# A decoder step on one core: decode states kept outside the weight ring and stored from GpSimd's queue, the last expert pair peeled, the final norm done tile by tile

## What is computed

```python
h = rms_norm(x, norm_mix); proj = h @ w_in
# 8 heads of gated DeltaNet: S_t = exp(g_t)(I - beta_t k_t k_t^T) S_{t-1} + beta_t k_t v_t^T, o_t = S_t^T q_t
# 8 heads of stick-breaking attention over the paged cache
x = x + concat(o_gdn, o_sb) @ w_out
logits = rms_norm(x, norm_ffn) @ router_w + router_b          # 32 experts, top 4, softmax gates
hu   = t[tok] @ w_up[e] + b_up[e]                             # 1024 -> 2048, gate and up interleaved
act  = (clip(up, -7, 7) + 1) * min(gate, 7) * sigmoid(1.702 * gate)
x = x + sum over experts of gate_e * (act @ w_down[e] + b_down[e])
y = x * rsqrt(mean(x * x) + eps) * norm_final                 # 256 prompt rows and 32 decode rows
```

## Time and profile before

| | us |
|---|---|
| median of 3 runs | 1422.4 |
| lowest, highest | 1418.89, 1425.12 |
| the profiled execution, its own time | 1421.34 |
| its span, first to last instruction | 1419.6 |
| PE busy in it | 1274.5 (90%) |
| DVE, ACT, POOL busy | 409.4, 257.7, 71.4 |
| HBM read, written | 459.67 MB, 3.70 MB |

### The profile page before, as it was taken

The page is one execution under the profiler, slowest core; times in us unless marked ns, Lnnn a source line. Parts: engine busy times, 40 slices in busy tenths (PEclk is TensorE's granted clock), DMA queues, the critical chain, the costliest instruction groups (busy, mean ns, idle before and its releaser), DMA issues. The chain is left out here.

```text
span 1419.6 us, 19928 instructions
## 1 busy us (share of the span) xinstructions
PE 1274.5 (90%) x7806; PEld 578.5 (41%) x7806; DVE 409.4 (29%) x930; ACT 257.7 (18%) x417; POOL 71.4 (5%) x124
## 2 busy tenths in 40 slices
PE   3999667697996899999999999999999999999995
PEld 3777454466944233333333333333333333333332
DVE  1740222245354223221322213222131221312223
ACT  2211291132222111010110201101011110111102
POOL 1400020003220000000000000000000000000000
PEclk8999897887997899999999999999999999999998
DMA  9444366861007799999999999999999999999993
GB/s 329 158 135 137 105 177 200 243 184 32 4 5 266 288 403 429 428 428 429 428 428 428 428 429 428 428 429 428 428 428 428 428 428 428 428 429 428 428 429 125
DMA packets 68787, 464.04 MB, mean 327 GB/s; under 512 B 16653, under 2 KB 16781, under 8 KB 44164
## 3 DMA queue, kind: packets, MB, share of 16 engines
q1 hardware_dynamic: 68740, 463.40, 80.8%
HBM read 459.67 MB, written 3.70 MB: 326 GB/s over the span
## 5 line engine op out<-in xcount | busy, mean ns | idle before, releaser
L1860 PE MATMUL bank<-ring,work 128*64 128x512 f32 x2048 | 451.0, 595 | 23.2 <-DMA ring<-in_w_up 23.2
L1860 PEld LDWEIGHTS bank<-ring,work 128*64 128x64 f32 x2048 | 149.1, 137 | 323.1 <-issue 323.1
L1877 PE MATMUL bank<-ring,work 128*64 128x512 f32 x1024 | 229.9, 597 | 10.8 <-DMA ring<-in_w_down 6.7
L1877 PEld LDWEIGHTS bank<-ring,work 128*64 128x64 f32 x1024 | 69.4, 137 | 149.5 <-issue 122.6
L404 PE MATMUL bank<-hT,ring 128*128 128x288 f32 x448 | 115.4, 415 | 11.2 <-PEq L263 10.6
L404 PEld LDWEIGHTS bank<-hT,ring 128*128 128x128 f32 x448 | 85.4, 194 | 34.7 <-issue 12.2
L2020 DVE TENSOR_SCALAR work<-bank 128x512 f32<-128x512 f32 x32 | 21.9, 685 | 257.8 <-PE bank L1860 257.8
L1935 ACT ACTIVATE work<-bank 128x1024 f32<-128x1024 f32 x16 | 16.4, 1024 | 392.1 <-PE bank L1814 392.1
L1992 DVE TENSOR_TENSOR X<-X,bank 128x512 f32<-128x512 f32 x68 | 46.8, 689 | 126.3 <-PE bank L1831 126.3
L2032 DVE COPY work<-bank 128x512 f32<-128x512 f32 x16 | 11.1, 692 | 215.3 <-PE bank L1877 215.3
L1831 PE MATMUL bank<-work 128*128 128x512 f32 x136 | 62.9, 605 | 0.9 <-ACT work L1961 0.9
(11 more groups left out here) (372 smaller groups left out, 1132.1 us busy)
## 6 DMA issues: line engine op xcount, KB each, us to landing
ring<-in_w_up SPq DMA_DIRECT2D x128, 2048.0 KB, 17.2
ring<-in_w_down SPq DMA_DIRECT2D x64, 2048.0 KB, 15.3
ring<-in_cache_k SPq DMA_DIRECT2D x64, 256.0 KB, 2.9
ring<-in_cache_v SPq DMA_DIRECT2D x64, 256.0 KB, 2.9
ring<-in_w_in SPq DMA_DIRECT2D x7, 2048.0 KB, 14.4
ring<-in_w_out SPq DMA_DIRECT2D x2, 2048.0 KB, 12.8
out<-work SPq DMA_DIRECT2D x4, 512.0 KB, 2.8
X<-in_x_prompt SPq DMA_DIRECT2D x1, 1024.0 KB, 5.1
```

The lines of the kernel that those rows point to most:

```text
L1860: ins = pe.matmul(bank[CAP * e:CAP * e + CAP, g, :], xT[:, k, CAP * e:CAP * e + CAP], weight(ch + e, k % 2 * RSLOT + 512 * g), start=False ...
L1877: ins = pe.matmul(bank[CAP * e:CAP * e + CAP, 4 + m, :], aT[:, k, CAP * e:CAP * e + CAP], weight(ch + e, k % 4 * D + 512 * m), start=False ...
```

## The change

In the mixer section `vm` moves out of the ring to a place in `work`, over constants that are not needed any more (`blk64`, which is, changes places with them), and the new decode states are written there too (`S1`), over the `vm` of the heads already used; the old states stay in the ring and are only read. SyncE's list loses the wait for `d_up`, the sixteen stores and the wait for them.

```diff
@@ -1030,15 +1030,16 @@
         assert f_ <= CONST_END, (f_, CONST_END)
         QK, wT, vn = (work[:, W * i:W * (i + 1)] for i in range(3))
         osq, ors, otm = Lb, Y, kbg
-        vm = ring[:, W:W + 2048].rearrange("p (h s d) -> p h s d", h=HP, s=NSEQ)
-        s_ssm = sem("ssm_stored")
+        vm = work[:, CONST_END:CONST_END + 2048].rearrange("p (h s d) -> p h s d", h=HP, s=NSEQ)
+        S1 = vm
+        s_ssm, s_sst = sem("ssm_prompt_stored"), sem("ssm_sample_stored")
...
                 sp.wait_ge(d_nrm, 3)
-                sp.wait_ge(d_up, 8)
                 for ch in range(2):
                     load_chunk(sp, 0, ch)
                 sp.wait_ge(s_ringfree, U_END)
                 for ch in range(4, NBUF):
                     load_chunk(sp, 0, ch)
                 sp.wait_ge(d_Sout, 4)
-                for par in range(2):
-                    for s in range(NSEQ):
-                        sp.dma_start(ssm_sample[0, s].rearrange("(p two) k v -> two k p v", two=2)[par],
-                                     S0[HD * par:HD * par + HD, s]).then_inc(s_ssm, 16)
-                sp.wait_ge(s_ssm, 32 + 256)
                 load_chunk(sp, 0, 2)
...
-                    dve.tensor_tensor(S0[:, :, p, :], S0[:, :, p, :], bank[:, 2 * (p % 2), :].rearrange("p (s d) -> p s d", s=NSEQ), ALU.add)\
+                    dve.tensor_tensor(S1[:, p], S0[:, :, p, :], bank[:, 2 * (p % 2), :].rearrange("p (s d) -> p s d", s=NSEQ), ALU.add)\
                        .then_inc(d_Sout, 1)
```

```diff
-                for ch in range(NBUF, CH):
+                for ch in range(NBUF, CH - 2):
                     sp.wait_ge(s_wused, CH * (NPAIR - 1) + ch - NBUF + 1)
                     load_chunk(sp, NPAIR - 1, ch)
+                for half in range(2):
+                    for ch in (CH - 2, CH - 1):
+                        if half == 0:
+                            sp.wait_ge(s_wused, CH * (NPAIR - 1) + ch - NBUF + 1)
+                        lo = (ch % NBUF) * 2 * RSLOT + half * RSLOT
+                        src = w_down[0, 2 * (NPAIR - 1) + ch % 2:2 * (NPAIR - 1) + ch % 2 + 1]\
+                            .rearrange("o (h p k) n -> p (o h) (k n)", h=2, k=4)[:, 1, half * RSLOT:(half + 1) * RSLOT]
+                        sp.dma_start(ring[:, lo:lo + RSLOT], src).then_inc(s_slot[2 * (ch % NBUF) + half], 16)
...
+                sp.wait_ge(s_nrow, 6 + 1)
+                sp.dma_start(y_sample.rearrange("s i d -> (s i) d"), yrow(2)).then_inc(s_yout, 16)
+                sp.wait_ge(s_nrow, 6 + 2)
+                sp.dma_start(y_prompt[0, toks(0), :], yrow(0)).then_inc(s_yout, 16)
+                sp.wait_ge(s_nrow, 6 + 4)
+                sp.dma_start(y_prompt[0, toks(1), :], yrow(1)).then_inc(s_yout, 16)
+                sp.wait_ge(s_ssm, 32)
+                sp.wait_ge(s_sst, 256)
+                sp.wait_ge(s_yout, 48)
...
-                pool.memset(oo, 0.0).then_inc(M["ready"], 1)
+                pool.memset(oo, 0.0).then_inc(d_pool, 1)
+                for s in range(NSEQ):
+                    for par in range(2):
+                        pool.dma_start(ssm_sample[0, s].rearrange("(p two) k v -> two k p v", two=2)[par],
+                                     S1[HD * par:HD * par + HD, :, s]).then_inc(s_sst, 16)
...
+                def down(i, q, in_halves=False):
 
                     ch = 8 + q // 2 * 2
-                    if q % 2 == 0:
+                    if in_halves and q == 3:
+                        for e in range(2):
+                            u = 2 * ((ch + e) % NBUF) + 1
+                            pe.wait_ge(s_slot[u], before[u] + 16)
+                    elif q % 2 == 0:
...
-                    down(i, 2)
-                    down(i, 3)
-                n = expert_loops(pe, body)
-                pe.wait_ge(M["xT_copied"], 2 * (n * NPAIR) + 2)
-                combine(n * NPAIR)
+                    down(i, 2, in_halves)
+                    down(i, 3, in_halves)
+
+                n = pe.value_load(npass[0:1, 0:1], min_val=1, max_val=-(-T // CAP))
+                with pe.Fori(0, NPAIR - 1) as j:
+                    body(j)
+                body(NPAIR - 1, True)
+                with pe.If(n > 1):
+                    with pe.Fori(1, n) as p:
+                        with pe.Fori(0, NPAIR) as j:
+                            body(p * NPAIR + j)
...
+                for m in range(2):
+                    ins = pe.matmul(bank[ND * m:ND * m + ND, 0, :], PGT[:, 2 * P:2 * P + ND], oo[:, 512 * m:512 * (m + 1)],
+                                    start=True, stop=True)
+                ins.then_inc(M["y"], 1)
+                pe.wait_ge(M["xT_copied"], 2 * i + 2)
+                for n in range(4):
+                    t, m = n // 2, n % 2
+                    pe.matmul(bank[:, 4 + n, :], PGT[:, t * P:(t + 1) * P], oo[:, 512 * m:512 * (m + 1)],
+                              start=True, stop=True).then_inc(M["y"], 1)
...
+                n = expert_loops(act, body)
+                act.activation(stat[:, 0, 1:2], stat[:, 0, 0:1], ACT.Sqrt)
+                for q, t in enumerate((2, 0, 1)):
+                    r = rows(t)
+                    for m in range(2):
+                        act.wait_ge(M["y_added"], 5 * n * NPAIR + 2 * q + m + 1)
+                        act.activation(ab[r, 512 * m:512 * (m + 1)], X[r, t, 512 * m:512 * (m + 1)], ACT.Square,
+                                       accum_out=fstat[r, t, m:m + 1]).then_inc(s_nsq, 1)
+                    act.wait_ge(s_nsq, 6 + 2 * q + 2)
+                    act.wait_ge(s_fin, FIN[f"shifted{q}"])
+                    act.activation(fstat[r, t, 3:4], fstat[r, t, 1:2], ACT.Sqrt, scale=1.0 / D, bias=fstat[r, t, 2:3]).then_inc(s_nstd, 1)
+                    if t == 1:
+                        act.wait_ge(s_fin, FIN["rstd2"])
+                        act.activation(yrow(t)[:, 512:D], yrow(t)[:, 512:D], ACT.Copy, scale=fstat[r, t, 4:5]).then_inc(s_nrow, 1)
...
+                def scale_rows(q):
+                    t = (2, 0, 1)[q]
+                    r = rows(t)
+                    dve.wait_ge(s_nstd, 6 + q + 1)
+                    dve.reciprocal(fstat[r, t, 4:5], fstat[r, t, 3:4]).then_inc(s_fin, 1)
+                    dve.wait_ge(s_fin, FIN[f"rstd{q}"])
+                    cols = slice(0, 512) if t == 1 else slice(0, D)
+                    dve.tensor_scalar(yrow(t)[:, cols], yrow(t)[:, cols], fstat[r, t, 4:5], None, ALU.mult).then_inc(s_nrow, 1)
...
+                base = 5 * nn * NPAIR
+                for q, t in enumerate((2, 0, 1)):
+                    r = rows(t)
+                    for m in range(2):
+                        dve.wait_ge(M["y"], base + (1 if t == 2 else 2 * t + m + 2))
+                        x = X[r, t, 512 * m:512 * (m + 1)]
+                        src = bank[ND * m:ND * m + ND, 0, :] if t == 2 else bank[:, 4 + 2 * t + m, :]
+                        dve.tensor_tensor(x, x, src, ALU.add).then_inc(M["y_added"], 1)
+                        if q and m == 0:
+                            scale_rows(q - 1)
+                    dve.wait_ge(M["y_added"], base + 2 * q + 2)
+                    dve.wait_ge(s_wb, 48)
+                    ins = dve.tensor_tensor(yrow(t), X[r, t, :], wb[r, :], ALU.mult)
+                    ins.then_inc(s_fin, 1)
+                    dve.wait_ge(s_nsq, 6 + 2 * q + 1)
+                    dve.tensor_scalar(fstat[r, t, 2:3], fstat[r, t, 0:1], 1.0 / D, EPS, ALU.mult, ALU.add).then_inc(s_fin, 1)
+                scale_rows(2)
```

More of the change, by code:

```diff
@@ L1106, in build @@
                  "aT_turned", "aT_copied", "out_copied_act", "out_copied_dve", "PG_turned", "PGT_copied", "y",
-                 "y_added", "dve_links", "picked", "picks_used", "ready")
+                 "y_added", "dve_links", "picked", "picks_used")
         M = {k: sem("moe_" + k) for k in names}
@@ L1370, in _ @@
                 turn_row(1, 0)
-                pe.wait_ge(s_rw, 32)
+                pe.wait_ge(s_rw, 128)
                 logits(0, 2)
@@ L1727, in _ @@
                 residual(1, 2)
-                dve.wait_ge(s_rw, 32)
+                dve.wait_ge(s_rw, 128)
                 choose(0, 2)
@@ L1759, in _ @@
                 dve_n[0] = c.n
+        yrow = lambda t: work[rows(t), D * t:D * (t + 1)]
+        fstat = sb("fstat", [P, 3, 5])
+        s_yout = sem("y_stored")
+        s_fin = sem("final_by_vector")
+        FIN = {n: i + 1 for i, n in enumerate(("weighted0", "shifted0", "rstd0", "weighted1", "shifted1", "rstd1", "weighted2",
+                                               "shifted2", "rstd2"))}
         before = [slot_count(max(u for u in range(U_END) if (u + 10) % NSLOT == i)) for i in range(NSLOT)]
@@ L1886, in turn_act, with body @@
                     ins.then_inc(M["aT_turned"], 1)
-                pe.wait_ge(M["ready"], 1)
-                pe.wait_ge(s_bias, 96)
-                def body(i, j):
+                pe.wait_ge(d_pool, SCALED["outputs_cleared"])
+                pe.wait_ge(s_bias, 128)
```

(29 more changed lines are left out.)

12 lines of the change are left out of this document (7 added, 5 removed).

## The result

The changed kernel takes 1412.5 us in the median of 6 runs (1409.7 to 1415.6), the kernel before 1421.9 in 6 runs beside it (1418.5 to 1425.1). The ratio is 0.9933, 95% interval 0.9914 to 0.9952: faster by 0.5 to 0.9%. The profiled execution took 1413.7 us, span 1412.0.

What follows compares the result with a forecast made beforehand. The weight stream was taken to bound the middle, SyncE's late arrival at the meeting the head, and serial work the tail. Gains of 7.3 + 0.4 + 1.6 = 9.3 us gave 1412.5 us, range 1408 to 1419.

Steps and rivals of the forecast that it cites:

- Bound and head: Meeting before the expert section: SyncE alone holds it; without its stores and waits TensorE starts 7.3 us earlier, at 458.3.
- The up to 1 us that I thought might come back there: TensorE's first 32 multiplications, 8.05 against 7.09: with shorter idleness ahead up to 1 us may return; taken as 0.
- It reaches the end: Weight stream behind TensorE's start: it resumes at TensorE's pace, so all 7.3 us pass on to the end.
- Stores: Sixteen state stores on GpSimd's queue from about 457: 1.47 us an issue, issues end at 481, cost taken as 0.
- the cover: Early pairs: stores' traffic falls half in idle DMA time, half beside chunks 6 and 7, landing before they are wanted.
- A: Rival in the early pairs: the stores run into the full stream, up to 5.0 us comes back, 1417.5; chance 0.14.
- The uncovered price of 5.0: Stores' traffic of 1.05 MB: 5.0 us of all DMA engines, the cost if nothing covered it.
- Halves: Last pair, peeled, last two chunks in half-size DMAs: TensorE's wait of 0.44 us goes, gain taken as 0.4.
- Norm: Tail, final norm by tile: combine to end of span 16.3 against 17.9 us, gain 1.6 (0.2 to 2.5).
- Sum: Whole kernel: 7.3 + 0.4 + 1.6 = 9.3 us, giving 1412.0 or 1413.1, forecast 1412.5.

Runs made afterwards that it cites:

- head_only: Kernel before with only states and masked v out of the ring, SyncE's two waits gone, stores on GpSimd's queue; 1415.6 us, ratio 0.9960.
- sync_stores_in_stream: Changed kernel with the sixteen state stores on SyncE's queue behind the eighth pair's loads, in the full stream; 1418.7 us, ratio 0.9981 to before.
- stores_on_sync: Changed kernel with the sixteen stores on SyncE's queue in the mixer section behind chunk 2, no wait for landing; 1410.6 us, ratio 0.9923 to before.

## Why the prediction was right

- **Bound and head.** SyncE held the meeting. Forecast 7.3, measured 7.2 in the changed kernel and 7.1 in head_only. TensorE's start was put at 458.3 and came at 459.7, which is the mixer section's 1.9 less 0.4 of a shorter gap (2.68 where I had kept 3.1). That 0.4 went back in the first stage, 8.58 against 8.05. The up to 1 us that I thought might come back there didn't: behind the pause of 3.4 us the granted clock was 0.50, 1.2 GHz, from 458 to 464.
- **It reaches the end.** The loads' spacing is the same to 0.01 us, and the stretch to the last combine to 0.2.
- **Stores.** GpSimd took 0.62 an issue and 10.07 for all, not 1.47 and 23.5: my value was SyncE's mean with its long stops in it, and the cover was ample. A did not happen: the last issue ended at 468.6, no DMA packet ran from 470 to 471, and the first freed load was issued at 470.42. The uncovered price of 5.0, which A rested on, holds for SyncE's short packets (5.0 above) and was carried over to a queue that sends others, where it was 2.6 to 2.9.
- **Halves.** The wait of 0.44 went, and the last pair is 0.7 shorter. In the time it can't be seen, because the stretch ahead of that pair, bound by the stream, was 0.8 longer in the changed kernel's profile (870.0 us from the first freed load, 869.2 in before, 869.4 to 869.8 in the runs without stores in the stream).
- **Norm.** Forecast 1.6, measured 2.5. The mis-sized terms: the last store was issued 12.0 behind the combine, not 13.2. Weighting took 1.22, not 1.28, the small operations some 0.15, not 0.2, scaling 0.75 (I had 0.7). VectorE's adds began at 1.08, not 1.3. In eight places the next instruction on VectorE begins 0.07 to 0.09 before the earlier one's row ends. The last half row took 0.49 on VectorE but 0.72 on ScalarE, which set the last store; I had 0.6 for both. The end behind that store was 3.4, not 3.1.
- **Sum.** 9.3 forecast; 9.4 by medians; by rows 7.2 for the head, 0.7 for the last pair and 2.5 for the tail, less the 0.8 ahead of the last pair, some 9.5. So two terms were too small by 1.2 together, and most of that was hidden by the 0.8, where the forecast took the stream's length as unchanged. The time of 1412.5, forecast and measured, agrees to 0.1 us by luck: it was set between 1412.0 and 1413.1, and one execution varies by 3.

## What to carry to other kernels

Where sections end with a meeting of all engines, look for the one that comes last and for what it does there: here a queue issued stores whose landing nothing needed but one buffer. The gain was passed on in full, even to a stretch that is bound by transfers, because these started again at the pace of the engine that was released. Ask which queue a small store stands in: between the loads of the full stream the same sixteen cost 7.4 us on SyncE's queue and 2.6 on GpSimd's, and where the engines had room no cost showed. And a share of busy time read in a quiet stretch is no price for another queue, nor for a busy one.

## What the runs showed of the hardware

- GpSimd's queue sends these stores (runs of 256 bytes) in few packets. The page's queue table after; before had no q0, and 68740 packets on q1:

```profile
q1 hardware_dynamic: 64676, 462.35, 80.8%
q0 software_dynamic: 512, 1.05, 0.5%
```

- 512 packets for 1.05 MB, but not of 2 KB each: in the rows from 462 to 470 above, 208 of 409 are under 512 bytes and the other 201 carry the 0.82 MB, 4 KB each. With the same stores on SyncE's queue (sync_stores_in_stream) the whole run has 16685 packets under 512 bytes, 4096 more than the changed kernel's 12589.
- These packets took 6.5 us of all engines in the quiet stretch (worked out above from 0.82 MB) and 2.9 in the full stream.
- One of its issues takes as long as an unhindered one on SyncE's queue (0.62), and in the quiet stretch it landed after 2.2 us in the median, where SyncE's in before landed after 3.3 in the median and 2.1 at the least. In the full stream GpSimd's sixteen issues still took 10.05 us, and landed after 10.9 in the median. Issues of GpSimd's stores after (ns, least, median, most; then landing in us):

```profile
L1821 POOL DMA_DIRECT2D out<-work x16: 622/622/847, 458.5 to 468.0; - x16
...
DMA to landing us min/median/max: 2.1/2.2/2.6
```

- SyncE's queue stopped in each run where these stores followed chunks of 2 MB: the longest issue took 9.12 us in before, 3.0 in stores_on_sync and 8.5 in the full stream, and all sixteen 23.5, 15.7 and 26.0, where a median issue took 0.62. How much the queue holds was not measured.
- Scaling 1024 columns of float32 by a per-row scalar took 0.75 us where weighting them by a tile took 1.22.
